# Token block sums in the layer before, weight sums ahead of the first eviction, first down weights as slots come free

## The chip, the cores and the metric

One NeuronCore of a Trainium2 chip. The metric is the device time of one execution in microseconds; the kernel before has a median of 3389.93 us over 3 runs (3389.51 to 3396.35). TensorE is PE in the profile, VectorE DVE, ScalarE ACT, GpSimd POOL, SyncE SP.

## The reference, cut to what matters

A stack of four transformer-like layers over 512 tokens of width 1024, in float32. Layers 0 and 1 are a mixer, a cross attention and a SwiGLU feed-forward network (FFN); a third layer (s) has another mixer and its own SwiGLU FFN; a fourth (t) has none. The part that the change touches:

```
def _swiglu(h, w_in, w_out):
    a, g = jnp.split(h @ w_in, 2, axis=-1)
    return (jax.nn.silu(a) * g) @ w_out
...
        x = x + _cross_attention(_rmsnorm(x, norm_xattn[l]), mem_n, xa_wq[l], xa_wkv[l], xa_wo[l])
        x = x + _swiglu(_rmsnorm(x, norm_ffn[l]), ffn_w_in[l], ffn_w_out[l])
```

The hidden width is 2816, that is 22 tiles of 128 (NH).

## The kernel before

Activations lie transposed, 8 tiles of 128 features by 512 tokens (X). Every float32 operand is split into a high part (rounded to fp32r) and the remainder, and a product is three matmuls: high x high, high x low, low x high (`unit_passes`, lines 318 to 320). Weights come in 527 units of 128 x 1024 through a ring of four raw tiles (RW, loaded by SP). ScalarE rounds a unit into WH (line 313, `w_hi`), GpSimd forms the remainder WL (line 3666), and WH and WL have three slots each (SPLIT). `w_hi(act, st, v)` rounds all units up to v that are not yet rounded; each waits for its raw tile and for its slot (`split_free`).

Each engine walks one list of stages in order (PLAN), so what stands behind a waiting instruction on its engine waits too. The stages around the change, for the FFN of layers 0 and 1 (f0, f1):

- `Linear("x0.o")` or `("x1.o")`: the output projection of the cross attention, 8 units j = 0 to 7, 24 matmuls each. VectorE adds each result into X ("eviction j", line 473); ScalarE squares X[j] (line 423), VectorE sums the squares (line 436).
- `Late`: ScalarE scales X by the norm's gain into XH (line 1234), VectorE forms XL (line 1244) and adds the last square (line 1254). The norm's reciprocal root is applied later, to the products.
- `Pairs(f.up, 2)`: the first two of 22 gate and up pairs, four ordinary units. The first starts tile by tile as XL comes (`pe_start`). Then the variance is summed on TensorE (line 1267), ScalarE takes the root (line 1276), VectorE the reciprocal (line 1284), scales each product (line 550) and multiplies gate by up (line 574, the "eviction" of a pair); ScalarE's SiLU is line 535.
- `Sevens`: the other 20 pairs by a scheme of Winograd's kind. The contraction is cut in two halves of 512 features, the tokens in two halves of 256 columns, a pair of weight units in the blocks A11, A12, A21, A22. Seven products per pair (A11, S1, S2, S4, S3, A12, A22, each 12 matmuls of 256 columns) replace eight. S1 to S4 are sums of weight blocks: VectorE forms S1, S2, S4 in PSUM banks 4 to 6 (`sums`, lines 788 to 792), GpSimd S3 in TERM (line 771). Each of the seven weight operands is rounded by ScalarE (line 759, `term_hi`); GpSimd forms the remainder of A11, S3, A12, A22 (line 774) and VectorE of S1, S2, S4 (line 779, `remainder`). The token operands of four products are sums of blocks of X (MIXED): `opening` on VectorE and `opening_act` on ScalarE form them, in two halves h of the contraction, each half as four sums `mix(t)` (line 690), four roundings (line 702) and four remainders (line 706, `mix_lo`). Half 0 needs X tiles 0, 1, 4, 5 and half 1 tiles 2, 3, 6, 7. Both halves stand at the head of `Pairs`, ahead of the root and the reciprocal. The weight sums of the first pair stand behind the first eviction of `Pairs` (`between(0)`), their remainders behind the second (`between(1)`). The bank of A11's result frees with the first eviction.
- `Down`: 22 units, each 24 matmuls over all eight banks. Its first units are rounded in `Sevens.scalar`: `ahead(m)` calls `w_hi` at m = 2 and 4 of the last pair, and once more stands behind the last SiLU. In `w_hi`, a unit of `Sevens` at index 3 or later returns at once (`if u - s7.u0 >= SPLIT: return`), and `st.unit`, the next unit to round, is moved past `Sevens` only behind the last SiLU.

The FFN of layer s (fs) has the same stages, except that its norm stands ahead (`late` is None): both halves of the sums stand at the head of `Pairs` too, and no reciprocal follows.

## Time and profile before

| | |
|---|---|
| median of 3 runs | 3389.93 us (3389.51 to 3396.35) |
| the profiled execution's own time | 3390.47 us |
| its span | 3388.7 us |
| TensorE busy | 3247.2 us, 96% |
| VectorE, ScalarE, GpSimd busy | 1720.6, 1424.4, 1447.8 us |
| mean granted clock | 0.986 |

Full speed of the clock (1.0) is 2.4 GHz, 0.5 is 1.2 GHz. Times in the rows are microseconds from the start of the span. In a timeline a row is the start, the duration, the engine, the line, the operation, output<-inputs, the shape and a count; in brackets stands how long the engine sat idle before and what released it. A row with a count over 1 runs from the start of its first to the end of its last instruction. TensorE's matmuls overlap, so the step from start to start is their pace (0.227 us for 512 columns and 0.12 for 256 at full clock), not the duration.

### The profile page before, as it was taken

Reading aid. Unit: us, or ns where it says so; the run is one execution under the profiler, and the core shown is the slowest. Engines: PE = TensorE matmul, PEld = TensorE weight load, DVE = VectorE, ACT = ScalarE, POOL = GpSimd, SP = SyncE. Lnnn points to the kernel's source line nnn. Section 1 sums busy time; section 2 is a strip of 40 time slices with the busy share of each in tenths; the row PEclk is TensorE's granted clock in tenths of the full one; section 3 lists DMA queues with packets and bytes.
Section 4 is the critical chain, followed back from the end, with each engine's and each line's share of the span. In section 5 each row is a group of like instructions: output and inputs, shape, how many; then the busy total and the mean of one; then the engine's idle time right before and its main releaser. Section 6 shows DMA issues by size and latency. Waiting matters only on the chain.

```text
span 3388.7 us, 47037 instructions
## 1 busy us (share of the span) xinstructions
PE 3247.2 (96%) x19536; PEld 2709.5 (80%) x19536; DVE 1720.6 (51%) x2631; ACT 1424.4 (42%) x2372; POOL 1447.8 (43%) x735
## 2 busy tenths in 40 slices
PE   8999989999999989999999998999899999999998
PEld 6778789987778789886677876998688778878887
DVE  8953478614443478513447655772373261134733
ACT  4543455423353455424434434553335432242332
POOL 5744256543354256543243023664344324414443
PEclk9999999999999999999999999999999999999999
DMA  4222123322232123333123031333232213212231
GB/s 165 87 94 94 50 81 107 104 96 94 69 106 94 50 82 112 101 100 104 55 84 117 20 107 63 109 104 100 81 118 94 69 56 100 87 38 97 96 124 69
DMA packets 83036, 302.88 MB, mean 89 GB/s; under 512 B 9060, under 2 KB 10888, under 8 KB 81928
## 3 DMA queue, kind: packets, MB, share of 16 engines
q1 hardware_dynamic: 78368, 280.55, 25.0%
q10 hardware_dynamic: 4456, 19.33, 1.5%
q8 instruction: 155, 2.54, 0.3%
q14 instruction: 57, 0.47, 0.0%
HBM read 290.39 MB, written 9.44 MB: 88 GB/s over the span
## 4 chain that ended last, share of the span: by engine, by line
PE 83%; DVE 8%; ACT 4%; issue 1%; POOL 0%; DVEq 0%; ACTq 0%
PE PS L318 23%; PE PS L319 22%; PE PS L320 22%; PE PS L1505 2%; PE PS L619 2%; PE PS L621 2%; PE PS L620 2%; PE PS L1626 1%; PE PS L2616 1%; DVE XL L1244 1%; DVE PS L690 1%; ACT WH L313 1%; PE PS L2608 1%; PE PS L1315 1%; PE PS L1491 1%
## 5 line engine op out<-in xcount | busy, mean ns | idle before, releaser
L3666 POOL TENSOR_TENSOR WL<-RW,WH 128x1024 fp32r<-128x1024 f32 x407 | 1005.2, 2473 | 1684.6 <-ACT WH L313 1684.1
L318 PE MATMUL PS<-XH,WH 128*128 128x512 f32 (+1 forms) x2728 | 1002.6, 368 | 50.8 <-POOL WL L774 16.5
L319 PE MATMUL PS<-XL,WH 128*128 128x512 f32 (+1 forms) x2728 | 993.0, 364 | 0.0
L320 PE MATMUL PS<-XH,WL 128*128 128x512 f32 (+1 forms) x2728 | 992.7, 364 | 0.0
L313 ACT ACTIVATE WH<-RW 128x1024 fp32r<-128x1024 f32 x407 | 427.0, 1053 | 590.1 <-PE PS L320 493.3
L318 PEld LDWEIGHTS PS<-XH,WH 128*128 128x128 f32 x2728 | 520.2, 191 | 152.1 <-issue 24.3
L320 PEld LDWEIGHTS PS<-XH,WL 128*128 128x128 f32 x2728 | 519.8, 191 | 80.2
L319 PEld LDWEIGHTS PS<-XL,WH 128*128 128x128 f32 x2728 | 520.4, 191 | 78.7 <-issue 2.2
L318 PE MATMUL PS<-YH,WH 128*128 128x512 f32 (+1 forms) x928 | 352.0, 379 | 17.8 <-POOL WL L3666 14.5
L319 PE MATMUL PS<-YL,WH 128*128 128x512 f32 (+1 forms) x928 | 350.8, 378 | 0.0
L320 PE MATMUL PS<-YH,WL 128*128 128x512 f32 (+1 forms) x928 | 350.3, 377 | 0.0
L318 PE MATMUL PS<-MIXED,WH 128*128 128x256 f32 x960 | 274.8, 286 | 6.7 <-DVE WL L779 6.7
L320 PE MATMUL PS<-MIXED,WL 128*128 128x256 f32 x960 | 274.4, 286 | 0.0
L319 PE MATMUL PS<-MIXED,WH 128*128 128x256 f32 x960 | 274.4, 286 | 0.0
L774 POOL TENSOR_TENSOR WL<-RW,WH 128x512 fp32r<-128x512 f32 x180 | 234.5, 1304 | 55.3 <-ACT WH L759 50.2
L318 PEld LDWEIGHTS PS<-YH,WH 128*128 128x128 f32 x928 | 176.5, 190 | 52.4 <-POOL WL L3666 17.6
L320 PEld LDWEIGHTS PS<-YH,WL 128*128 128x128 f32 x928 | 176.9, 191 | 31.7
L319 PEld LDWEIGHTS PS<-YL,WH 128*128 128x128 f32 x928 | 176.8, 190 | 31.1
L318 PEld LDWEIGHTS PS<-MIXED,WH 128*128 128x128 f32 x960 | 186.8, 195 | 7.5 <-DVE WL L779 7.5
L319 PEld LDWEIGHTS PS<-MIXED,WH 128*128 128x128 f32 x960 | 186.9, 195 | 0.0
L320 PEld LDWEIGHTS PS<-MIXED,WL 128*128 128x128 f32 x960 | 186.9, 195 | 0.0
L950 DVE TENSOR_TENSOR YL<-A,YH 128x512 fp32r<-128x512 f32 x66 | 47.9, 737 | 272.7 <-ACT YH L946 272.7
(583 smaller groups left out, 4436.8 us busy)
## 6 DMA issues: line engine op xcount, KB each, us to landing
RW<-in_units SPq DMA_DIRECT2D x527, 512.0 KB, 3.3
spill<-X ACTq DMA_DIRECT2D x2, 2048.0 KB, 6.6
X<-in_xT SPq DMA_DIRECT2D x8, 256.0 KB, 6.2
A<-spill ACTq DMA_DIRECT2D x1, 2048.0 KB, 7.8
X<-spill ACTq DMA_DIRECT2D x4, 512.0 KB, 5.7
X<-spill ACTq DMA_DIRECT2D x1, 2048.0 KB, 9.3
out_T<-X ACTq DMA_DIRECT2D x4, 512.0 KB, 3.0
spill<-X ACTq DMA_DIRECT2D x1, 1536.0 KB, 5.1
```

What stands on the lines that cost most here:

```text
L313: nc.scalar.activation(WH[:, u % SPLIT, :], RW[:, u % RAW, :], ACT.Copy).then_inc(split_hi, 1)
L318: mm(out, hi, xh, start=first, stop=False, skip_group_check=onto)
L319: mm(out, hi, xl, start=False, stop=False, skip_group_check=onto)
L320: return mm(out, lo, xh, start=False, stop=last, skip_group_check=onto)
L619: mm(o, xh, wh, start=(k == 0), stop=False)
L620: mm(o, xh, wl, start=False, stop=False)
L621: last = mm(o, xl, wh, start=False, stop=(k == KT - 1))
L690: st.do(nc.vector.scalar_tensor_tensor(out=self.part(out, h, k), in0=self.x(half, cols, k), scalar=self.gain_of(half, k), in1=self.part(ot ...
L774: nc.gpsimd.tensor_tensor(WLH[:, w, :], self.raw(p, m), WHH[:, w, :].bitcast(F32), ALU.subtract).then_inc(term_done, 1)
L950: st.do(nc.vector.tensor_tensor(YL[:, self.hslot(k), :], T(k), YH[:, self.hslot(k), :].bitcast(F32), ALU.subtract), f"{self.name}.lo{k}")
L1505: last = mm(PS[rows, 6 + n % 2, c0:S], value(j), self.pt_of(s, g)[:, j, c0:S], start=(j == 0), stop=(j == (TT if self.keys is None else se ...
L3666: nc.gpsimd.tensor_tensor(WL[:, u % SPLIT, :], RW[:, u % RAW, :], WH[:, u % SPLIT, :].bitcast(F32), ALU.subtract).then_inc(split_done, 1)
```

## The change

1. In layers 0 and 1, half 0 of the token block sums is formed in the `Linear` before, behind evictions 5 and 6 (`early`, `early_act`, hung on `outs[l].between` and `between_act`). The squares of that layer go to tiles 8 to 15, since the old ones lie under MIXED. In fs, `early` stays at the head of `Pairs`.
2. Half 1 is `finish`: at the head of `Pairs` in layers 0 and 1, behind the first eviction in fs. S1, S2, S4 of the first pair are formed in `finish` too: behind the root in layers 0 and 1, ahead of the reciprocal. The remainders of S1 and S2 stand behind the first eviction, that of S4 behind the second.
3. ScalarE rounds A11 and S1 ahead of the first pair's SiLU (`amid_act` is set, so `w_hi` is called ahead of it).
4. `st.unit` is moved past `Sevens` inside `ahead`, so the calls at m = 2 and 4 of the last pair round down units 0 and 1.

```
@@ Linear.vector @@
                     st.do(ins, f"ev{self.e0 + j}")
+                    if self.between is not None:
+                        self.between(st, j)
@@ Pairs.scalar @@
                         if self.of:
                             w_hi(act, st, u + SPLIT + self.eager)
+                        elif self.amid_act is not None:
+                            w_hi(act, st, u + SPLIT + (i == 0))
                         st.wait_ge(*reached(f"gated{e}"))
...
+                    if self.amid_act is not None:
+                        self.amid_act(st, i)
@@ Sevens @@
+            def early(self, st, j):
+                if j == 5:
+                    st.settle()
+                    self.mix(st, 0, 0)
+                    self.mix(st, 0, 1)
+                    self.mix_lo(st, 0, 0)
+                elif j == 6:
+                    st.settle()
+                    self.mix(st, 0, 2)
+                    self.mix(st, 0, 3)
+                    for t in (1, 2, 3):
+                        self.mix_lo(st, 0, t)
+
+            def early_act(self, st, j):
+                if j == 5:
+                    self.right_act(st, 0)
+                    self.mix_hi(st, 0, 0)
+                elif j == 6:
+                    for t in (2, 1, 3):
+                        self.mix_hi(st, 0, t)
+
+            def finish(self, st):
+                st.settle()
+                self.mix(st, 1, 0)
+                self.mix(st, 1, 1)
+                if self.late is None:
+                    self.sum_one(st, 0)
+                self.mix_lo(st, 1, 0)
+                st.settle()
+                self.mix(st, 1, 2)
+                self.mix(st, 1, 3)
+                for t in (1, 2, 3):
+                    self.mix_lo(st, 1, t)
+                if self.late is not None:
+                    st.wait_ge(*reached(f"{self.late.id}.std"))
+                    self.sum_one(st, 0)
+                self.sum_two(st, 0)
+                self.sum_four(st, 0)
+
+            def finish_act(self, st):
+                self.right_act(st, 1)
+                for t in (0, 2, 1, 3):
+                    self.mix_hi(st, 1, t)
...
             def opening(self, st):
-                for h in range(2):
-                    self.mix(st, h, 0)
-                    self.mix(st, h, 1)
-                    self.mix_lo(st, h, 0)
-                    st.settle()
-                    self.mix(st, h, 2)
-                    self.mix(st, h, 3)
-                    for t in (2, 1, 3):
-                        self.mix_lo(st, h, t)
-                    st.settle()
+                if self.late is None:
+                    for j in (5, 6):
+                        self.early(st, j)
+                else:
+                    self.finish(st)
...
+            def amid_act(self, st, i):
+                if i == 0 and self.late is None:
+                    self.finish_act(st)
+
             def between(self, st, i):
-                if i == 0:
-                    self.sums(st, 0)
-                elif i == 1:
+                if i == 0 and self.late is None:
+                    self.finish(st)
+                if i == self.first - 2:
+                    self.remainder(st, 0, self.S1)
+                    self.remainder(st, 0, self.S2)
+                elif i == self.first - 1:
+                    self.remainder(st, 0, self.S4)
                     if self.late is not None:
                         st.do(nc.vector.tensor_copy(bank(self.RSTD), self.late.r))
-                    for m in (self.S1, self.S2, self.S4):
-                        self.remainder(st, 0, m)
@@ Sevens.scalar, ahead @@
                         elif m in (2, 4):
+                            st.unit = max(st.unit, self.u0 + 2 * self.n)
                             w_hi(act, st, self.u0 + 2 * self.n + m // 2 - 1)
@@ xattn @@
-            o = Linear(f"x{l}.o", add=True, ready=f"xo{l}", squares=20, summing=KT - 1)
+            o = outs[l] = Linear(f"x{l}.o", add=True, ready=f"xo{l}", squares=8, summing=KT - 1)
@@ ffn @@
+            if late is not None:
+                outs[l].between, outs[l].between_act = s7.early, s7.early_act
```

TensorE's, GpSimd's and SyncE's orders stay as they are. VectorE's order at the end of x0.o and the head of f0.up, before:

```order
L473 TENSOR_TENSOR X<-X,PS 128x512
L436 TENSOR_TENSOR SD<-SD,A 128x512
L1244 SCALAR_TENSOR_TENSOR XL<-X,VEC,XH 128x512 x4
L473 TENSOR_TENSOR X<-X,PS 128x512
L1244 SCALAR_TENSOR_TENSOR XL<-X,VEC,XH 128x512 x4
L1254 TENSOR_TENSOR SD<-SD,A 128x512
L690 SCALAR_TENSOR_TENSOR PS<-X,VEC,PS 128x256 x4
L706 TENSOR_TENSOR MIXED<-PS,MIXED 128x512
L690 SCALAR_TENSOR_TENSOR PS<-X,VEC,PS 128x256 x4
L706 TENSOR_TENSOR MIXED<-PS,MIXED 128x512 x3
```

The same place in the changed kernel, from eviction 5 on (line 690 is now 696, 706 is 713, 1244 is 1307):

```order
L473 TENSOR_TENSOR X<-X,PS 128x512
L696 SCALAR_TENSOR_TENSOR PS<-X,VEC,PS 128x256 x4
L713 TENSOR_TENSOR MIXED<-PS,MIXED 128x512
L436 TENSOR_TENSOR SD<-SD,A 128x512
L473 TENSOR_TENSOR X<-X,PS 128x512
L696 SCALAR_TENSOR_TENSOR PS<-X,VEC,PS 128x256 x4
L713 TENSOR_TENSOR MIXED<-PS,MIXED 128x512 x3
L436 TENSOR_TENSOR SD<-SD,A 128x512
L1307 SCALAR_TENSOR_TENSOR XL<-X,VEC,XH 128x512 x4
L473 TENSOR_TENSOR X<-X,PS 128x512
L1307 SCALAR_TENSOR_TENSOR XL<-X,VEC,XH 128x512 x4
```

Eight sums and four remainders stand between evictions 5 and 7 now. ScalarE's order from the root to the second SiLU in f0.up, before and then in the changed kernel (L1276 and L1339 are the root, L535 and L539 the SiLU, L759 and L813 the rounding of a weight operand: from RW it is A11, from PS S1, S2, S4):

```order
L1276 ACTIVATE NR<-PS,CST 128x512
L535 ACT_TABLE_LOAD
L535 ACTIVATE SG<-SG 128x512
L759 ACTIVATE WH<-RW 128x512
L759 ACTIVATE WH<-PS 128x512
L535 ACTIVATE SG<-SG 128x512
```

```order
L1339 ACTIVATE NR<-PS,CST 128x512
L813 ACTIVATE WH<-RW 128x512
L813 ACTIVATE WH<-PS 128x512
L539 ACT_TABLE_LOAD
L539 ACTIVATE SG<-SG 128x512
L813 ACTIVATE WH<-PS 128x512 x2
L539 ACTIVATE SG<-SG 128x512
```

A11 and S1 moved ahead of the first SiLU. ScalarE's order at the end of `Sevens` in f0, before and then in the changed kernel (L853 and L916 are the last copy of a result, L859 and L922 the last SiLU, L313 the rounding of down units):

```order
L853 ACTIVATE SG<-PS 128x256
L859 ACTIVATE SG<-SG 128x512
L313 ACTIVATE WH<-RW 128x1024 x3
```

```order
L916 ACTIVATE SG<-PS 128x256
L313 ACTIVATE WH<-RW 128x1024 x2
L922 ACTIVATE SG<-SG 128x512
L313 ACTIVATE WH<-RW 128x1024
```

Two of the three roundings moved ahead of the last SiLU. The same rows stand in f1 and fs.

## Rows read from the trace of the kernel before

**Rows 1.** The page, part 1: busy us, share of the span, instructions.
```profile
PE 3247.2 (96%) x19536; PEld 2709.5 (80%) x19536; DVE 1720.6 (51%) x2631; ACT 1424.4 (42%) x2372; POOL 1447.8 (43%) x735
```

**Rows 2.** Waits of TensorE: us in total, times, longest us.
```profile
PE PS L318 <- POOL WL L3666: 17.2, 9, 3.9
PE PS L318 <- POOL WL L774: 16.5, 3, 7.5
...
PE PS L318 <- DVE WL L779: 6.7, 3, 2.3
```

**Rows 3.** Timeline of TensorE, head of f0's seven-product stage: start, duration, instruction, idle before.
```profile
438.94 0.39 PE L320 MATMUL PS<-XH,WL 128*128 128x512 f32 x1
446.80 0.58 PE L318 MATMUL PS<-XH,WH 128*128 128x256 f32 x1 [7.46 <-POOL WL L774]
...
452.06 0.58 PE L318 MATMUL PS<-MIXED,WH 128*128 128x256 f32 x1 [2.34 <-DVE WL L779]
```

**Rows 4.** Windows: length, busy us (count) of PE, PEld, DVE, ACT, POOL; granted clock; DMA.
```profile
443.50:444.00 0.50, 0.00 (x0) 0.00 (x0) 0.50 (x1) 0.00 (x0) 0.00 (x0) 0.76 0.00 0
457.00:457.50 0.50, 0.50 (x4) 0.50 (x4) 0.00 (x0) 0.00 (x0) 0.50 (x2) 0.59 0.71 131
...
2107.00:2110.00 3.00, 2.78 (x23) 2.78 (x24) 2.83 (x5) 2.54 (x6) 2.59 (x2) 1.00 0.00 0
```

**Rows 5.** Timeline of VectorE around the same head.
```profile
413.35 4.38 DVE L1244 SCALAR_TENSOR_TENSOR XL<-X,VEC,XH 128x512 fp32r<-128x512 f32 x4 [0.87 <-ACT XH L1234]
...
418.25 2.73 DVE L1244 SCALAR_TENSOR_TENSOR XL<-X,VEC,XH 128x512 fp32r<-128x512 f32 x4
421.08 2.71 DVE L1254 TENSOR_TENSOR SD<-SD,A 128x512 f32<-128x512 f32 x1
423.82 1.79 DVE L690 SCALAR_TENSOR_TENSOR PS<-X,VEC,PS 128x256 f32<-128x256 f32 x4
426.28 0.69 DVE L706 TENSOR_TENSOR MIXED<-PS,MIXED 128x512 fp32r<-128x512 f32 x1 [0.67 <-ACT MIXED L702]
...
439.99 3.35 DVE L1284 RECIPROCAL NR<-NR 128x512 f32<-128x512 f32 x1 [1.27 <-ACT NR L1276]
443.47 1.29 DVE L550 TENSOR_TENSOR SG<-PS,NR 128x512 f32<-128x512 f32 x2
444.93 0.69 DVE L574 TENSOR_TENSOR A<-SG 128x512 f32<-128x512 f32 x1 [0.17 <-ACT SG L535]
```

**Rows 6.** Timeline of ScalarE around the same head.
```profile
406.22 1.04 ACT L313 ACTIVATE WH<-RW 128x1024 fp32r<-128x1024 f32 x1
...
439.20 0.69 ACT L1276 ACTIVATE NR<-PS,CST 128x512 f32<-128x512 f32 x1
...
464.79 0.38 ACT L847 ACTIVATE SG<-PS 128x256 f32<-128x256 f32 x1 [0.29 <-PE PS L320]
...
474.87 0.38 ACT L847 ACTIVATE SG<-PS 128x256 f32<-128x256 f32 x1 [0.29 <-PE PS L320]
```

**Rows 7.** Timeline of GpSimd around the same head.
```profile
420.77 2.47 POOL L3666 TENSOR_TENSOR WL<-RW,WH 128x1024 fp32r<-128x1024 f32 x1 [5.58 <-ACT WH L313]
```

**Rows 8.** Timeline of ScalarE, last pair of f0's seven-product stage.
```profile
649.11 0.39 ACT L853 ACTIVATE SG<-PS 128x256 f32<-128x256 f32 x1 [1.06 <-PE PS L320]
...
655.15 2.93 ACT L313 ACTIVATE WH<-RW 128x1024 fp32r<-128x1024 f32 x3
```

**Rows 9.** Timeline of TensorE, the same place.
```profile
654.55 0.28 PE L320 MATMUL PS<-MIXED,WL 128*128 128x256 f32 x1
658.69 0.72 PE L318 MATMUL PS<-YH,WH 128*128 128x512 f32 x1 [3.86 <-POOL WL L3666]
```

**Rows 10.** Timeline of VectorE, the same place: the last eviction.
```profile
656.34 0.41 DVE L899 TENSOR_TENSOR A<-SG,PS 128x256 f32<-128x256 f32 x1
```

**Rows 11.** Windows, same columns: f0's down projection, its first products.
```profile
662.00:662.50 0.50, 0.50 (x3) 0.36 (x3) 0.00 (x0) 0.00 (x0) 0.50 (x1) 0.79 1.02 205
```

**Rows 12.** Timeline of TensorE, first product of fs.down.
```profile
2310.74 0.72 PE L318 MATMUL PS<-YH,WH 128*128 128x512 f32 x1 [3.11 <-POOL WL L3666]
```

More of the change, by code:

```diff
@@ L699, in mix_act, with mix_hi @@
                     st.do(nc.scalar.activation(self.part(self.MIX_BANK[3], h, k), self.x(0, 1, k), ACT.Copy, scale=self.gain_of(0, k)), f"{self.name}.right{h}")
-                for t, read in ((0, 1), (2, 2), (1, 3), (3, 3)):
-                    st.wait(f"{self.name}.mix{read}.{h}")
-                    st.do(nc.scalar.activation(self.mixed_half(t, h, 0), bank(self.MIX_BANK[t]), ACT.Copy), f"{self.name}.mixhi{t}.{h}")
+            def mix_hi(self, st, h, t):
+                st.wait(f"{self.name}.mix{(1, 3, 2, 3)[t]}.{h}")
+                st.do(nc.scalar.activation(self.mixed_half(t, h, 0), bank(self.MIX_BANK[t]), ACT.Copy), f"{self.name}.mixhi{t}.{h}")
             def mix_lo(self, st, h, t):
@@ new lines, in finish_act @@
+            def finish_act(self, st):
+                self.right_act(st, 1)
+                for t in (0, 2, 1, 3):
+                    self.mix_hi(st, 1, t)
+            def opening(self, st):
+                if self.late is None:
[3 more added lines that the diff above has]
+                    self.finish(st)
+            def opening_act(self, st):
+                if self.late is None:
+                    for j in (5, 6):
+                        self.early_act(st, j)
+                else:
+                    self.finish_act(st)
@@ L1634, in xattn @@
             split(f"xo{l}", [T(28 + k) for k in range(KT)], XH, XL, ready=lambda k: f"xa{l}.o{k}")
-            o = Linear(f"x{l}.o", add=True, ready=f"xo{l}", squares=20, summing=KT - 1)
-            o.then = late(f"fn{l}", f"norm_ffn{l}", ready=lambda k: f"ev{o.e0 + k}", after=o.name, left=[KT - 1], sq=lambda i: T(20 + i))
+            o = outs[l] = Linear(f"x{l}.o", add=True, ready=f"xo{l}", squares=8, summing=KT - 1)
+            o.then = late(f"fn{l}", f"norm_ffn{l}", ready=lambda k: f"ev{o.e0 + k}", after=o.name, left=[KT - 1], sq=lambda i: T(8 + i))
             return o.then
@@ L1641, in keys @@
             return T(((14, 15, 36, 37), (4, 5, 6, 7))[l][j // 2])[:, (j % 2) * MEM:(j % 2 + 1) * MEM]
-        mix = {}
+        mix, outs = {}, {}
         def ffn(l, alpha=None, late=None, summed=False, weights=None, first=1):
@@ L1648, in ffn @@
             s7 = up.sevens = Sevens(f"f{l}.up", 2, NH - 2, at(0), ACT.Silu, None if late is None else f"norm_ffn{l}", late, f"fn{l}.biased7" if late is None else None)
-            up.opening, up.opening_act, up.between = s7.opening, s7.opening_act, s7.between
+            up.opening, up.opening_act, up.amid_act, up.between = s7.opening, s7.opening_act, s7.amid_act, s7.between
+            if late is not None:
+                outs[l].between, outs[l].between_act = s7.early, s7.early_act
             s7.then = Down(f"f{l}.down", up, alpha, summed, weights)
```

35 lines of the change are left out of this document (19 added, 16 removed).

## The prediction

> **What bounds the kernel now.** I read the page's busy shares first, then the waits of TensorE, then the timelines and clock windows at the two ends of the seven-product stages. TensorE is busy for 96% of the span [rows 1], so time is won only by closing its gaps, or by keeping its clock up. Nearly all of the largest gaps fed by GpSimd lie at two kinds of places, and the diff touches both [rows 2]. The first is the head of `Sevens`, where the first product (A11) waits for WL of line 774 (16.5 us in three waits, one in each FFN layer) and the second (S1) for the remainder of line 779 (6.7 us in three). The second is the head of `Down`: waits of 3.9 us in f0 and f1 (the longest of line 3666), and 3.11 us in fs [rows 12].
>
> In f0 the last matmul of the four up units starts at 438.94, A11 at 446.80 after 7.46 us idle, S1 at 452.06 after 2.34 more [rows 3]. The granted clock falls near 443.6 (0.76 is the mean of a half window at 2.4 GHz and at 1.2) and is back only near 457.3 [rows 4]. ScalarE's first copy of a pair comes right behind that pair's A11: 464.79 and 474.87 [rows 6], so a pair takes 10.08 us on TensorE. The second pair's A11 therefore started one seventh of 10.08 (1.44 us) before 464.7, at 463.3. From 438.94 to 463.3 are 24.4 us, for 10.1 of products: 7.9 us of step to A11, 2.3 of wait at S1, and 4.1 lost to the clock.
>
> Why A11 is late: VectorE works without a long pause from 413 to 445 (lows, both halves of the block sums, the reciprocal of 3.35 us, two scalings 1.29, the eviction at 444.93) [rows 5]. A11's weights were rounded by ScalarE only behind the first pair's SiLU, although they were in the raw ring long before.
>
> **The change, part by part: head of f0.** I carry the new order forward with before's durations.
>
> 1. Half 0 of the block sums goes behind evictions 5 and 6 of x0.o. ScalarE's rounding behind eviction 5 starts at 406.22 and occupies it to 407.2 [rows 6]; the two gain products then take 0.86, so VectorE starts at 408.1. One step (four 256-column sums, round, remainder) takes 3.15 us, from 423.82 to the end of 426.28+0.69 [rows 5], so to 411.3. The square sum and eviction 6 end at 412.6, the next four sums at 414.4, and the three remainders, since the new order asks for the one that ScalarE rounds second first, at 417.3. Then come a square sum (417.9), four lows at 0.68 each (420.7), eviction 7 (421.3) and four lows of 2.73 in all [rows 5], ending at 424.0; before they ended at 421.0. So the first up unit, which eats one low per 0.68 us, starts 2.8 us late, at 418.6, and ends **3.0 us later**, at 424.7. This is the price of the change.
>
> 2. VectorE's last square sum then meets GpSimd's WL of the third unit. Before, this sum took 2.71 us and ended 0.55 after GpSimd's 420.77+2.47 [rows 5, 7], while the sums of line 690, which read PSUM and one SBUF tile, ran 1.79 for four. So operations of VectorE with two SBUF operands wait for GpSimd here. It now ends at 426.8. The GPSIMD Engine Reference of the Trainium skill (Specifications) states the same, contention for the shared SBUF interfaces with VectorE instructions that have two SBUF inputs; by that rule, the trace agrees, and the moved sum S1 (two raw weight tiles) is exposed to it as well. A sum without it would put the reciprocal some 2 us earlier and be about 2 us better per layer.
>
> 3. Half 1 follows, 3.15 + 4.4 us, to 434.4. ScalarE rounds unit four (432.9, behind all of half 1, where before it stood between the halves), GpSimd takes some 2.4 [rows 7] and the fourth unit can start at 436.5, just 0.3 late. The square root follows the rounding and a table load of 1.3 us: it ends at 435.9 (439.9 before [rows 6]).
>
> 4. The weight sums S1, S2, S4 stand ahead of the reciprocal now: S1 waits for GpSimd until 436.5 and ends at 437.0, the others at 438.4. The reciprocal of 3.35 ends at 441.8 (443.3 before), so it gains little. The scalings take 1.29, and the eviction ends at 443.9 (445.6 before) [rows 5].
>
> 5. A11 no longer waits for the SiLU: rounded at 436.5, its WL is done at 439.5 behind GpSimd's TERM. What is late next is its bank, which frees with the first eviction: **A11 starts at 443.95**. TensorE ends unit four at 442.0, so it idles 2.0 us. S1's remainder follows the eviction directly, 444.6, and waits for nothing. S2 needs ScalarE's copy of A11, queued behind the second SiLU and two roundings: 1.1 us idle. The second pair starts at 443.95+10.08+1.1 = 455.1.
>
> 463.3 - 455.1 = **8.2 us in f0**. The same by terms: 7.9+2.3+4.1 go, 3.0+2.0+1.1 (and rounding) come. This takes the clock as staying up: in fs, behind idle of 1.6 and 2.0 us, it stood at 1.00 [rows 4]. The idle at the head of the up stage is 3.0 us, and could lower it there; but 0.9 us lost in unit one is covered by the 2.0 at A11. f1 has the same shape (its wait is the 7.5 of rows 2): 8.2 again. Bounds for a layer: 5 (the clock falls, another 1.8, and S1 or S2 slip by 1.4) and 10.2 (no idle at A11).
>
> **Head of fs.** This layer has no preceding `Linear` to take half 0. Half 1 goes behind the first eviction. Its waits are 16.5 less twice 7.5, 1.6 us, and 6.7 less 2.34 twice, 2.0. Unit four's weights are now rounded behind a table load and a SiLU, so that unit starts 1.6 late, in place of the 1.6 at A11; the sums are ready sooner, so most of the 2.0 goes. I take 2.0, bounds -1 and 3.6.
>
> **Tail of the seven-product stages.** ScalarE is done with its copies at 649.5 and then has only the last SiLU until 655.15, where the three roundings of down units stand in a row [rows 8]. The last product's last matmul starts at 654.55, the first of down at 658.69 [rows 9]. Now units 0 and 1 are rounded behind products 3 and 5 of the last pair. Unit 0: 649.4 to 650.4, GpSimd to 652.9, two us before TensorE asks; unit 1 is done at 655.5. Its lows are there, and the banks of the first nine passes are free; the next three (asked for at 656.7) want the last weighting, the others (at 657.4) the last eviction, which ends at 656.75 behind it [rows 10], so both come in time. So the step of 4.14 us becomes 0.12: 4.0 us. The clock fell during that gap and was back near 662.2 [rows 11]: 3.5 us at half rate, 1.8 to 1.9 us. **5.9 us each in f0 and f1**, bounds 4.0 and 5.9. In fs the wait is 3.11 [rows 12]: 3.3 + 1.7 = 5.0. GpSimd's WL of unit 1 may hold an eviction there by 1 us; down's banks 4 to 7 cover it with 2.7 us of passes.
>
> Down units 1 and 2 are ready in time, and everything behind shifts with TensorE. Instruction counts of TensorE, GpSimd and the DMA queue stay as they are; the squares move to other tiles at no cost.
>
> **Sum.** 2 x 8.2 + 2.0 + 2 x 5.9 + 5.0 = 35.2 us. The profiled execution took 3390.5 us (span 3388.7 and 1.8 around it), 0.5 above the median of the runs: 3390.5 - 35.2 = 3355.3, and I say 3355.
>
> **The rivals.**
> A: the heads pay less, since the clock falls in the new gaps after all. For it: the wait of 3.9 us at down's head was enough [rows 9, 11], and the new gaps are 3.0 and 2.0. Against: fs [rows 4]. Price 1.8 per fall plus slips, 2 to 4 in each of f0 and f1: 3359 to 3363. The page TensorE: Matmul & The Clock Gate of the Trainium skill (Why this matters for your kernels) warns of idle gaps between bursts of matmuls for this reason.
> B: the heads pay nothing. Half 1, the weight sums and the reciprocal stand in one VectorE queue; if the early half costs more than the 3.0 us (evictions 6 and 7 held longer), the first eviction is no earlier than before and the gap just moves. Then only the tails pay, 16.8: 3374.
> C: the tails pay nothing, because the early roundings delay the copies and SiLU of the last pair or their raw tiles have not landed. ScalarE's free time from 649.5 on speaks against [rows 8]. Only the heads pay, 18.4: 3372.
> D, slower: the clock falls in the 3.0 us gap at the up stage and stays at 1.2 GHz through its four units. That is 4 x 24 matmuls of 0.227 us = 21.8 us more per layer, 43.6 for two, less the 35.2: 3399. It decides from 17.6 us of work at half rate per layer on. Low stretches here last 3.5 to 13.7 us, the latter with two further gaps inside [rows 3, 4, 11], which speaks against it.
>
> **How the numbers follow.** Forecast 0.68, A 0.20, B 0.06, C 0.04, D 0.02. The forecast's own range: heads 2 x (-2 to +2), fs head -3 to +1.6, tails to -4: 3349 to 3362 as a practical spread. With A it reaches 3364; B and C are left out, most of the 2 in 10, and I add 2 us for phases of the clock elsewhere that shift: 3347 to 3366. About 0.2% (7 us) is what this measurement can tell from no change. Forecast, A, B and C are all faster by more than that: 0.97, with 0.01 for the same (both B and C) and 0.02 slower.
>
> **What would show it.** The waits of TensorE on line 774's successor should fall from 16.5 to under 5 us, those at down's head be gone, the step to the first product of down be 0.12 us. The first up unit of f0 should start near 418.6 (a new wait of 3 us on VectorE's XL), A11 near 444, the second pair near 455, with the clock at 1.00. I am wrong if A11 starts after 446, if the clock falls there, or if down's head still shows a gap.

## The result and the profile after

| | before | after |
|---|---|---|
| median | 3390.44 us (3389.51 to 3396.35, 4 runs) | 3359.67 us (3358.76 to 3360.74, 4 runs) |
| the profiled execution's own time | 3390.47 us | 3360.74 us |
| its span | 3388.7 us | 3358.9 us |

The ratio is 0.9906, 95% interval 0.9889 to 0.9923: 30.8 us faster, where 35.2 were summed. The range, 3347 to 3366, held it; rival A's, 3359 to 3363, holds it as well, so the time alone does not choose between the forecast and A. A second measurement of the same kernel (below) gave 3357.78 us.

The page of the changed kernel, part 1, answers to [rows 1]:

```profile
PE 3239.8 (96%) x19536; PEld 2700.3 (80%) x19536; DVE 1716.6 (51%) x2631; ACT 1424.4 (42%) x2372; POOL 1450.7 (43%) x735
```

The same instructions, and on every engine nearly the same busy time. What went is idle time of TensorE. Its waits, as in [rows 2] (us in total, times, longest; L3731 was L3666, L833 was L779, L1307 was L1244, L580 was L574):

```profile
PE PS L318 <- DVE XL L1307: 21.2, 10, 10.0
...
PE PS L318 <- POOL WL L3731: 6.6, 6, 2.2
PE PS L318 <- DVE A L580: 3.6, 2, 1.8
...
PE PS L318 <- DVE WL L833: 1.1, 2, 0.7
```

The 16.5 us of line 774 are gone, and 10.6 of the 17.2 us of line 3666. New are 3.6 us for the first eviction, and the waits on XL (15.7 us in six on line 1244 before) are longer by about the 2.85 us in each of f0 and f1 that step 1 asked for.

**Head of f0.** Timeline of TensorE (start, duration, instruction, idle before and its releaser), against [rows 3]:

```profile
419.81 0.47 PE L318 MATMUL PS<-XH,WH 128*128 128x512 f32 x1 [2.85 <-DVE XL L1307]
...
442.85 0.39 PE L320 MATMUL PS<-XH,WL 128*128 128x512 f32 x1
445.06 0.36 PE L318 MATMUL PS<-XH,WH 128*128 128x256 f32 x1 [1.82 <-DVE A L580]
```

Timeline of VectorE, against [rows 5]:

```profile
413.81 1.80 DVE L696 SCALAR_TENSOR_TENSOR PS<-X,VEC,PS 128x256 f32<-128x256 f32 x4
416.38 1.89 DVE L713 TENSOR_TENSOR MIXED<-PS,MIXED 128x512 fp32r<-128x512 f32 x3 [0.78 <-ACT MIXED L709]
...
425.00 2.70 DVE L1317 TENSOR_TENSOR SD<-SD,A 128x512 f32<-128x512 f32 x1
...
436.83 1.00 DVE L839 SCALAR_TENSOR_TENSOR PS<-RW 128x512 f32<-128x512 f32 x1 [1.55 <-ACT NR L1339]
...
439.28 3.35 DVE L1347 RECIPROCAL NR<-NR 128x512 f32<-128x512 f32 x1
442.76 1.29 DVE L556 TENSOR_TENSOR SG<-PS,NR 128x512 f32<-128x512 f32 x2
444.22 0.69 DVE L580 TENSOR_TENSOR A<-SG 128x512 f32<-128x512 f32 x1 [0.17 <-ACT SG L539]
```

Timeline of GpSimd and of ScalarE, against [rows 7] and [rows 6]:

```profile
424.70 2.46 POOL L3731 TENSOR_TENSOR WL<-RW,WH 128x1024 fp32r<-128x1024 f32 x1 [6.84 <-ACT WH L313]
```

```profile
458.33 0.39 ACT L910 ACTIVATE SG<-PS 128x256 f32<-128x256 f32 x1 [0.29 <-PE PS L320]
```

Half 0 now stands between evictions 5 and 7, the first up unit waits 2.85 us, the square sum is held by GpSimd for 2.70 us again (it ends at 427.70, 0.54 after GpSimd's 424.70+2.46), and A11 waits for its bank. The second pair's first copy came at 464.79 and comes at 458.33.

**Tail of f0.** Timelines of ScalarE, GpSimd and TensorE, against [rows 8, 9]:

```profile
642.93 1.05 ACT L313 ACTIVATE WH<-RW 128x1024 fp32r<-128x1024 f32 x1
645.59 1.06 ACT L313 ACTIVATE WH<-RW 128x1024 fp32r<-128x1024 f32 x1 [1.61 <-PE PS L320]
648.16 0.63 ACT L922 ACTIVATE SG<-SG 128x512 f32<-128x512 f32 x1 [1.50 <-DVE SG L955]
```

```profile
644.06 5.07 POOL L3731 TENSOR_TENSOR WL<-RW,WH 128x1024 fp32r<-128x1024 f32 x2 [2.02 <-ACT WH L313]
```

```profile
648.09 0.28 PE L320 MATMUL PS<-MIXED,WL 128*128 128x256 f32 x1
648.21 0.40 PE L318 MATMUL PS<-YH,WH 128*128 128x512 f32 x1
```

Two units are rounded behind products of the last pair, GpSimd works on them while TensorE still multiplies, and the first product of down follows after 0.12 us, as forecast; the step was 4.14.

**An account by stages.** To see where time went, I take the same VectorE instruction in both traces, at a point before and a point behind each place, and subtract its times. How far the changed kernel is ahead, in us:

| place | ahead in front | ahead behind | won there | forecast |
|---|---|---|---|---|
| head of f0 | -1.2 | 6.4 | **7.6** | 8.2 |
| tail of f0 | 6.4 | 12.2 | **5.7** | 5.9 |
| head of f1 | 12.1 | 20.2 | **8.1** | 8.2 |
| tail of f1 | 20.2 | 25.9 | **5.7** | 5.9 |
| head of fs | 24.5 | 25.8 | **1.3** | 2.0 |
| tail of fs | 25.8 | 30.8 | **5.0** | 5.0 |
| sum | | | **33.4** | 35.2 |

The points are read to 0.1 us, so a row can be off by that.

What the places won is 33.4 us; the span is shorter by 29.8. The rest was given back between them, where no instruction was changed: 1.2 us before the first place (0.8 of it at 247 to 255 us, where the clock was low for 6.8 us, and before for 3.4), 1.4 between f1's tail and fs, in small steps that no single row explains, and 1.7 at 2650 to 2655 us of the changed kernel's trace, a low stretch that the kernel before did not have; 0.4 came back at the very end. This account holds for two executions. The interval of the ratio, 26 to 38 us, has room for 33.4 and for 35.2 as well.

### The profile page after: what moved, and what is told of

The parts are those of the page before. It is cut to its first block, busy times and chain, and to the rows that moved or that the text cites. A ratio compares the mean times of both kernels' runs of the same rounds, so it can differ in the third digit from the quotient of the medians.

```text
span 3358.9 us, 47090 instructions
## 1 busy us (share of the span) xinstructions
PE 3239.8 (96%) x19536; PEld 2700.3 (80%) x19536; DVE 1716.6 (51%) x2631; ACT 1424.4 (42%) x2372; POOL 1450.7 (43%) x735
## 4 chain that ended last, share of the span: by engine, by line
PE 83%; DVE 8%; ACT 3%; issue 1%; DVEq 0%; ACTq 0%
PE PS L318 23%; PE PS L320 22%; PE PS L319 22%; PE PS L1568 2%; PE PS L625 2%; PE PS L627 2%; PE PS L626 2%; PE PS L2681 1%; PE PS L1689 1%; PE PS L2673 1%; PE PS L1378 1%; PE PS L1554 1%; ACT WH L313 1%; DVE XL L1307 1%; PE PS L3357 1%
## 5 line engine op out<-in xcount | busy, mean ns | idle before, releaser
L3731 POOL TENSOR_TENSOR WL<-RW,WH 128x1024 fp32r<-128x1024 f32 x407 | 1006.5, 2476 | 1678.3 <-ACT WH L313 1677.8
L313 ACT ACTIVATE WH<-RW 128x1024 fp32r<-128x1024 f32 x407 | 427.7, 1054 | 593.5 <-PE PS L320 496.8
```

The source lines that it names most:

```text
L313: nc.scalar.activation(WH[:, u % SPLIT, :], RW[:, u % RAW, :], ACT.Copy).then_inc(split_hi, 1)
L3731: nc.gpsimd.tensor_tensor(WL[:, u % SPLIT, :], RW[:, u % RAW, :], WH[:, u % SPLIT, :].bitcast(F32), ALU.subtract).then_inc(split_done, 1)
```

## The experiments

In all the runs the kernel before was measured beside the others: 3392.1, 3391.81 and 3391.18 us for the three groups. Ratios are to it. "Head" and "tail" gains are by the account above. Theories of the expectations: A is the prediction's, B its rival.

**1. The tails alone** (the kernel before with one line):

```
                         elif m in (2, 4):
+                            st.unit = max(st.unit, self.u0 + 2 * self.n)
                             w_hi(act, st, self.u0 + 2 * self.n + m // 2 - 1)
```

> The kernel before with one line of the change: the unit counter is moved past the seven-product stage inside `ahead`, so that down units 0 and 1 are rounded behind products 3 and 5 of the last pair. My theory (each part pays where it stands): the tails alone give 5.7 us in f0, 5.75 in f1 and 5.2 in fs as the trace of the changed kernel shows, 16.7 in all, so 0.9951 of before (about 3373.7). The three steps to down's first matmul are 0.12 to 0.25 us and the clock stays at 1.00 there, while the waits of 7.5 us at the two heads stay. Rival (most of it is the heads, and the tails' gain is given back by clock falls elsewhere): under 12 us.

3379.52 us (3378.89 to 3380.97), ratio 0.9961 (0.9948 to 0.9973): 12.6 us faster, by the interval 9.2 to 17.6. By stages the three tails win 5.7, 5.7 and 5.0, 16.4 together: all of what was expected. Windows of its clock (length, busy us and count of PE, PEld, DVE, ACT, POOL, granted clock, DMA):

```profile
1618.00:1629.00 11.00, 10.09 (x32) 6.02 (x33) 7.76 (x20) 5.14 (x21) 0.00 (x0) 0.53 0.06 21
2096.00:2104.00 8.00, 6.07 (x33) 5.77 (x33) 5.57 (x9) 4.91 (x11) 5.08 (x4) 0.57 0.13 35
```

The second is the head of fs, which this edit leaves as it was, and where the clock of the kernel before stood at 1.00 [rows 4]: 2.0 us are lost there. The first costs 2.7. It goes the other way too: the head of f0 is not touched either, and there the clock was low for 6.8 us in place of 13.7, which gave 2.3 us. So the price of the tails was right, and its profiled execution (10.4 us shorter by span) is short of it by low clock elsewhere. The median, 12.6, lies between the expected 16.7 and the rival's "under 12", and its interval holds both; it is the stage gains that speak for the theory.

**2. The heads alone** (the changed kernel without that line):

> The changed kernel without that line: heads alone. Theory: 7.6 us in f0, 9.6 in f1, 0.8 in fs, 18.0 in all, 0.9947 of before; the waits of 3.9, 3.9 and 3.1 us at down's heads stand as before, and e1 and e2 add up to the whole change plus what the clock takes elsewhere (34.8 by stages against 29.8 in the spans). Rival (the two parts help each other, for example by the clock): their gains add up to clearly less than 30.8.

3377.8 us (3374.11 to 3381.07), ratio 0.9956 (0.9943 to 0.9968): 14.3 us faster, by the interval 11 to 19. The heads win 7.6, 8.1 and 1.3 us, 17.0 together; 9.6 had been expected for f1 and 0.8 for fs. The tails of f0 and f1 win nothing, and that of fs loses 1.2: the clock is low there for 6.8 us, before for 3.4. The stage gains of the two halves, 16.4 and 17.0, add up to the 33.4 of the whole; their medians do so only within their intervals (12.6 + 14.3 = 26.9, against 30.8). Rival C falls by run 1, rival B by this one.

**3. Half 0 back at the head of the up stage** in f0 and f1; the rest of the change stays:

```
             def opening(self, st):
-                if self.late is None:
-                    for j in (5, 6):
-                        self.early(st, j)
-                else:
+                for j in (5, 6):
+                    self.early(st, j)
+                if self.late is not None:
                     self.finish(st)
...
-            if late is not None:
-                outs[l].between, outs[l].between_act = s7.early, s7.early_act
```

(and alike for ScalarE, with unit four rounded between the halves)

> The changed kernel with half 0 of the token block sums of f0 and f1 put back to the head of the up stage (between the lows and half 1), all else kept: the first weight sums ahead of the reciprocal, A11 and S1 rounded ahead of the first SiLU. Theory A (VectorE's queue is what bounds the heads): half 0 costs VectorE some 7.5 us there, of which only the 3 us by which the first up unit starts sooner come back to TensorE, and these do not count since the fourth unit then only waits longer for the first eviction. The first eviction of f0 moves from 444.9 to about 449, A11 with it, idle before A11 8 to 9 us instead of 1.8, and the clock falls there: 5 to 7 us slower than the changed kernel in each of f0 and f1, 10 to 14 in all. Theory B (the early half gives nothing, the order at the first SiLU is what pays): within 3 us of the changed kernel.

3369.96 us (3367.8 to 3370.64), ratio 0.993 (0.9916 to 0.9943), 10.3 us slower than the changed kernel. TensorE at the head of f0:

```profile
449.06 0.55 PE L318 MATMUL PS<-XH,WH 128*128 128x256 f32 x1 [9.09 <-DVE A L580]
```

The heads of f0 and f1 lose 5.8 and 6.0 us against the changed kernel: theory A holds (5 to 7 in each), B is refuted. With the shift in front of the place taken off, A11 comes 4.5 us later in both layers; a low stretch of 10.2 us, where the changed kernel has 3.4 in f0 and none in f1, goes with the rest. These 4.5 us are the 7.5 us of half 0 less the 3.0 that step 1 had put as its price. The weight sums ahead of the eviction, without the early half, make A11's wait longer than it ever was (9.1 us against 7.5): they lengthen the queue of VectorE. The early half is what pays for them.

**4. Only part of half 0 early.** The sums behind eviction 6 are moved behind the lows; those behind eviction 5 stay.

```
+                if self.late is not None:
+                    self.early(st, 6)
...
-                outs[l].between, outs[l].between_act = s7.early, s7.early_act
+                outs[l].between = lambda st, j: s7.early(st, j) if j == 5 else None
+                outs[l].between_act = lambda st, j: s7.early_act(st, j) if j == 5 else None
```

(and alike for ScalarE, with unit four rounded ahead of half 1)

> The changed kernel with the second part of half 0 (four sums, three roundings, three remainders, about 4.4 us of VectorE) moved from behind eviction 6 to behind the lows in f0 and f1; the first part stays behind eviction 5. Theory A (VectorE's queue sets the first eviction, TensorE's 2.9 us of idle at the head of the up stage is covered): the idle at the up stage's head goes to about 0, but the work of VectorE between eviction 5 and the first eviction stays the same, so A11 moves by no more than 2 us either way and the idle there grows from 1.8 to about 4.5 us; the clock may fall for longer. Time within 4 us of the changed kernel, rather slower. Theory B (the late start of the up stage is a real price): 2 x 2.9 = about 6 us faster than the changed kernel.

3365.71 us (3365.17 to 3367.86), ratio 0.9921 (0.9907 to 0.9934), 6.0 us slower than the changed kernel: A's "rather slower" with a size beyond its 4, and B, faster, refuted. The up stage waits 1.59 us in place of 2.85, not about 0 as A had it, and A11 waits the more, 5.92 us where A said 4.5:

```profile
417.74 0.47 PE L318 MATMUL PS<-XH,WH 128*128 128x512 f32 x1 [1.59 <-DVE XL L1312]
...
447.10 0.55 PE L318 MATMUL PS<-XH,WH 128*128 128x256 f32 x1 [5.92 <-DVE A L580]
```

The 2.85 us wait in front of the up stage is worth its price: of the 4.4 us of VectorE's work that were moved to behind the lows, 2.8 reach A11 in both layers. The rest does not, since the lows, which start sooner, now meet GpSimd. VectorE and GpSimd here, and VectorE in the changed kernel:

```profile
415.22 4.36 DVE L1312 SCALAR_TENSOR_TENSOR XL<-X,VEC,XH 128x512 fp32r<-128x512 f32 x4 [0.87 <-ACT XH L1302]
```

```profile
414.65 2.39 POOL L3737 TENSOR_TENSOR WL<-RW,WH 128x1024 fp32r<-128x1024 f32 x1 [4.56 <-ACT WH L313]
```

```profile
418.92 2.74 DVE L1307 SCALAR_TENSOR_TENSOR XL<-X,VEC,XH 128x512 fp32r<-128x512 f32 x4
```

The first low ends 0.55 us after GpSimd's operation and takes 2.37 us of the 4.36, as the square sum is held in step 2 of the prediction; the same stood in the kernel before (4.38 us for four [rows 5]), and the early half takes the lows out of GpSimd's way. The heads lose 2.9 and 3.5 us.

**5. Sums S2 and S4 behind the first eviction** in f0 and f1:

```
-                self.sum_two(st, 0)
-                self.sum_four(st, 0)
+                else:
+                    self.sum_two(st, 0)
+                    self.sum_four(st, 0)
...
+                    if self.late is not None:
+                        self.sum_two(st, 0)
+                        self.sum_four(st, 0)
```

> The changed kernel with the second and third weight sum of f0's and f1's first pair (1.4 us of VectorE) moved from ahead of the reciprocal to behind the first eviction and the remainder of S1. Theory A (VectorE's queue bounds the whole head, not only A11): the first eviction comes 1.4 us sooner and the idle of 1.8 us at A11 shrinks to about 0.4, but the remainders of S2 and S4 come 1.5 us later than they would and TensorE waits there instead, 0.4 us at S2 and about 1.2 at S4: no gain in f1, and at most the 1.8 us of the clock in f0. Within 2 us of the changed kernel. Theory B (A11's bank is the only thing that is late): 1.4 us per layer, and the clock stays up in f0: 3 to 5 us faster.

3364.19 us (3362.19 to 3364.9), ratio 0.9917 (0.9902 to 0.9932), 4.5 us slower than the changed kernel by medians whose intervals overlap. A11 no longer waits, the third product (S2) does. TensorE and the first eviction on VectorE, and a window:

```profile
443.30 0.28 PE L318 MATMUL PS<-XH,WH 128*128 128x256 f32 x1
...
448.69 0.35 PE L318 MATMUL PS<-MIXED,WH 128*128 128x256 f32 x1 [2.36 <-DVE WL L838]
```

```profile
441.78 0.69 DVE L580 TENSOR_TENSOR A<-SG 128x512 f32<-128x512 f32 x1 [0.17 <-ACT SG L539]
```

```profile
420.00:424.00 4.00, 4.00 (x12) 3.12 (x11) 4.00 (x7) 2.80 (x5) 0.20 (x1) 0.57 0.01 4
```

That A11 does not wait at all is in part the clock's doing: it was low in the up stage in both layers, so TensorE came later to A11. The eviction ended 0.83 us ahead of A11, where 0.15 is the distance when A11 waits for it, so its bank was free 0.7 us before TensorE came. Where the changed kernel's clock fell at the same place, A11's wait was 1.1 us shorter for it (0.70 in place of 1.80, run 8), so with the clock up a wait of about 0.4 would have been left here (an estimate), as A had it. The wait at S2, 2.36 us, is above A's 0.4 there and 1.2 at S4 together; S4 waits for nothing.

By stages the two heads lose only 0.2 and 0.7 us, within A's 2 us. The profiled execution, the fastest of the four, is behind the changed kernel's by 1.5 us of span, 0.9 of it at these heads; the rest of the 4.5 us between the medians is not explained by the edit. That it would gain (B) is refuted.

**6 and 7. A short delay at the start.** The changed kernel with two (then four) copies of ScalarE put ahead of its first rounding, 1.1 (2.2) us, nothing else:

```
+                raw_landed(st, 0)
+                for k in range(2):
+                    nc.scalar.activation(SG[:, k, :], RW[:, 0, 0:S], ACT.Copy)
```

> The changed kernel with two extra ScalarE copies of 128x512 (1.1 us) ahead of the first rounding, so that all that follows starts 1.1 us later and nothing else is changed. Theory (where the clock falls among the gaps depends on when in the execution they lie; that took about 5 us of the 34.8 us that the stages gave): the time differs from the changed kernel by something else than 1.1 us, up to 6 us either way, and the low stretches lie at other gaps, while stage by stage the steps with the clock at 1.00 are the same. Rival (the clock falls at the same gaps whatever their time): 1.1 us slower within 1 us, same low stretches.

> The same with four copies, 2.2 us. Theory: again other low stretches, a time that does not follow the delay (between 3357 and 3367). Rival: 2.2 us slower than the changed kernel and 1.1 slower than the run before it, same low stretches.

3359.26 us (3358.25 to 3361.84), ratio 0.9902 (0.9886 to 0.9919), and 3361.74 us (3359.77 to 3362.61), ratio 0.991 (0.9895 to 0.9925). Against the trace of run 8 below, the same program without the copies, the first is 1.0 us late at 60 us, then 3.0 at 403, 4.6 at 805, 2.0 at 2060 and 1.8 at 3300; the second 2.0, 1.7, 3.8, 1.4 and 1.3. By medians the first is 0.4 us under the changed kernel's first result, where the rival had 1.1 above it within 1 us; the second is 2.1 above, the rival's 2.2, and 4.0 above run 8. The rival's "same low stretches" is refuted in both: the first trace has two, at 365.1 and 423.2 us, that neither trace of the changed kernel has. The delay is there at the start and then drowns in jumps of 1 to 3 us, up and down, which lie where one execution has a low stretch and the other none. Whether the delay itself chose these stretches, the two runs cannot say; run 8 shows that none is needed.

**8. The changed kernel once more**, unaltered:

> The changed kernel once more, unaltered, beside the three that follow on the same chip. Theory A (the changed kernel's own time repeats within about 2 us): 3358 to 3362, ratio to the kernel before 0.990 to 0.992. Theory B (a few us of every result are the accident of which gaps the clock fell in during one measurement, so that a repeat wanders too): more than 3 us away from 3359.7.

3357.78 us (3354.71 to 3359.92), ratio 0.9899 (0.9883 to 0.9916). By the median A holds (just under its range), but single executions of one unaltered program range over 5 us. Beside the kernel before in this group, 3391.18 us, the gain is 33.4 us, what the account by places had summed. Three stretches by window, first in the first trace of the changed kernel:

```profile
445.50:449.50 4.00, 4.00 (x23) 4.00 (x22) 3.73 (x8) 2.46 (x5) 1.53 (x2) 0.57 0.00 0
1162.00:1166.00 4.00, 3.84 (x18) 2.75 (x16) 3.95 (x7) 2.80 (x6) 0.24 (x1) 1.00 0.00 0
2039.00:2046.00 7.00, 4.98 (x15) 1.26 (x16) 5.30 (x9) 4.62 (x9) 2.49 (x1) 1.00 0.20 77
```

and in this one, the same program:

```profile
445.50:449.50 4.00, 3.33 (x28) 3.15 (x28) 3.72 (x7) 3.26 (x7) 2.06 (x2) 1.00 0.00 0
1162.00:1166.00 4.00, 4.00 (x13) 3.13 (x12) 4.00 (x7) 2.81 (x5) 0.02 (x1) 0.57 0.00 0
2039.00:2046.00 7.00, 5.74 (x16) 1.45 (x16) 4.72 (x8) 6.10 (x9) 0.77 (x1) 0.53 0.22 75
```

All three changed sides. (Run 8 was measured on the chip of runs 9, 10 and 12, the first trace in another measurement; that the chip alone does not decide it is seen on this chip itself, in the last section.) At 1162 to 1166 us the clock fell behind the new wait in front of f1's up stage, and it cost nothing: TensorE came later to A11 and waited less there, while A11 started at the same point of VectorE's order. TensorE in f1, the first trace and then this one:

```profile
1186.11 0.36 PE L318 MATMUL PS<-XH,WH 128*128 128x256 f32 x1 [1.80 <-DVE A L580]
```

```profile
1186.35 0.36 PE L318 MATMUL PS<-XH,WH 128*128 128x256 f32 x1 [0.70 <-DVE A L580]
```

In f0, where the clock stayed up this time, the third product (S2) shows the wait that the prediction had put at 1.1 us. TensorE, and ScalarE's copy of A11's result:

```profile
448.30 0.36 PE L318 MATMUL PS<-MIXED,WH 128*128 128x256 f32 x1 [0.67 <-DVE WL L833]
```

```profile
447.79 0.36 ACT L910 ACTIVATE SG<-PS 128x256 f32<-128x256 f32 x1
```

The row names a remainder of VectorE, but the one that ended last (448.24) is S4's, for which S2 does not wait. By the kernel S2 waits for ScalarE's copy, as the prediction said: it ends at 448.15, 0.15 us ahead of the product, the same distance as from the first eviction to A11.

With the clock low (the first trace) it is absent, since the products come later than their operands. So the fall in f0 costs only 0.5 us by the account, not the 1.7 of its 3.4 us at half rate. Run 10 has the same in f1: the clock fell behind A11 there, and by the account this head loses 0.5 us against the first trace.

**9. The remainders in another order** (2, 1, 3 in place of 1, 2, 3, in both halves):

```
-                    for t in (1, 2, 3):
+                    for t in (2, 1, 3):
                         self.mix_lo(st, 0, t)
```

> The changed kernel with only this altered: the remainders of the token block sums are formed in the order 2, 1, 3, so that block 2's, which A11's sum reads first, is there one VectorE operation sooner. By the stage account of the run with both edits, A11's wait at each FFN head falls from 1.8 to about 0.7 us: theory A, 1.5 to 3 us faster than the changed kernel, 3357 to 3358. Theory B (the 2.7 us between the changed kernel and that run were the clock's accident, not the edit): within 1 us of the changed kernel in this same call.

3357.69 us (3356.19 to 3360.88), ratio 0.9903 (0.9888 to 0.9918): the same as run 8. TensorE at f0's up stage and at A11:

```profile
418.76 0.47 PE L318 MATMUL PS<-XH,WH 128*128 128x512 f32 x1 [2.37 <-DVE XL L1307]
...
444.00 0.36 PE L318 MATMUL PS<-XH,WH 128*128 128x256 f32 x1 [1.82 <-DVE A L580]
```

My stage reading was wrong. The 0.7 us at A11, seen in the run with both edits, came of a fall of the clock at 422 to 426 in it, as in f1 of run 8. The order buys 0.5 us at the up stage of f0 and of f1 (2.37 against 2.85), because ScalarE rounds block 2 second, and by the account 0.6 us at the head of fs, where unit four waits 1.38 us in place of 1.69; 1.6 us in all is below what the medians tell.

**10. Unit four's weights early in fs:**

```
+                        if i == 0 and self.amid_act is not None:
+                            w_hi(act, st, u + SPLIT)
```

> The changed kernel with only this altered: in the last layer's second FFN stage (about 2100 us) the fourth up unit's weights are rounded by GpSimd before the first SiLU instead of amid the stage. Stage account: the wait of 1.7 us on that rounding before unit four goes and turns up at the first weight sum, so that the head pays nothing: theory A, 3359 to 3361, within 1 us of the changed kernel. Theory B (a wait on GpSimd costs only at unit four, the sum has slack): 1.4 to 1.7 us faster than the changed kernel, 3358.

3358.89 us (3356.22 to 3360.09), ratio 0.9904 (0.989 to 0.9919), the same again. The changed kernel waited for unit four's weights in fs:

```profile
2073.19 0.50 PE L318 MATMUL PS<-XH,WH 128*128 128x512 f32 x1 [1.69 <-POOL WL L3731]
```

Now A11 waits in its place, for GpSimd's remainder:

```profile
2076.60 0.39 PE L318 MATMUL PS<-XH,WH 128*128 128x256 f32 x1 [1.79 <-POOL WL L830]
```

Theory A in its sum: the wait taken from one product goes to another, and by the account the head loses 0.1 us. It goes to A11, though, which reads no weight sum, and not to the first weight sum as A had it; and it is ScalarE that rounds the unit, where the expectation says GpSimd. Both waits are on GpSimd's remainders, which speaks for its queue as the bound of this head.

**11 and 12. Both edits**, in the group of runs 5 to 7 and again beside run 8:

> The changed kernel with two edits: in all three FFN layers the block sums' remainders are formed in the order 2, 1, 3, in which ScalarE rounds them, in place of 1, 2, 3 (0.67 us less for VectorE at each of two places in f0 and f1 and two in fs); and in fs the fourth up unit is rounded ahead of the first SiLU and its table load. Theory A: VectorE's chain to the first eviction is 1.3 us shorter in f0 and f1, the idle at A11 goes from 1.8 to about 0.5 and the clock need not fall in f0; in fs the wait of 1.7 us for that unit's weights goes, and part of it comes back at A11 behind the shorter VectorE chain. Together 3 to 6 us faster than the changed kernel, less or more by what the clock does elsewhere. Theory B (these heads are bound by something else): no change beyond 1 us.

> Both edits once more (order 2, 1, 3 and the fourth unit's weights early), beside the changed kernel on the same chip. Theory A (the edit pays): 1.5 to 3.5 us below the changed kernel of this call, about 3357. Theory B: within 1 us of it.

3357.02 us (3355.96 to 3361.12), ratio 0.9899 (0.9884 to 0.9914), and 3358.25 us (3356.04 to 3360.47), ratio 0.9904 (0.9889 to 0.9918). The first lies 2.7 us under the first result of the changed kernel, and would pass for a gain; beside the changed kernel on one chip the second lies 0.5 us above it. Both theories A (3 to 6, then 1.5 to 3.5 us) fall. By stages the order's 0.5 us is there in f0 and fs of both, too small for the medians. No version was found that beats the changed kernel by more than the measurement tells.

## Why the prediction was right, step by step

- **Step 1** said that the early half costs 3.0 us in front of the up stage: the row says 2.85. The trace of after runs 1.2 us late from before this place on; with that taken off, the first product stands at 418.6, the time forecast. Without the early half, A11 is 4.5 us later (run 3), the 7.5 us of half 0 less that price, and with its second part behind the lows 2.8 (run 4).
- **Step 2**, the square sum held by GpSimd: 2.71 us before, 2.70 after. The comparison that the step drew, with the four sums of line 690, tests nothing: they start at 423.82, when GpSimd's operation had ended at 423.24. The changed kernel has rows that do, at the second pair, VectorE and then GpSimd:

```profile
449.48 1.65 DVE L839 SCALAR_TENSOR_TENSOR PS<-RW 128x512 f32<-128x512 f32 x1
451.24 0.70 DVE L844 SCALAR_TENSOR_TENSOR PS<-PS,RW 128x512 f32<-128x512 f32 x1
```

```profile
449.28 2.99 POOL L828 TENSOR_TENSOR WL<-RW,WH 128x512 fp32r<-128x512 f32 x2
```

  Both sums ran while GpSimd worked; S1's, of two SBUF tiles, took 1.65 us, and S2's, of PSUM and one SBUF tile, 0.70. In the first pair S1's sum took 1.00, and 0.70 in run 4, where GpSimd was idle for most of it: held a little, as the step said. What it waited for is ScalarE's root (idle of 1.55 us), where step 4 had named GpSimd.
- **Step 3**, the root's end at 435.9: ScalarE's row ends at 436.80, less 1.2 is 435.6.
- **Step 4**, the reciprocal's end at 441.8: 442.63 less 1.2 is 441.5. **Step 5**, A11 at 443.95 behind the first eviction: 445.06 less 1.2 is 443.9, idle 1.8 where 2.0 was said. That the bank bounds A11 is shown by the distance from the end of the first eviction to A11's start, 0.15 us in both layers of both traces and of runs 3 and 4, whose waits are 9.1 and 5.9 us; in run 5, where the eviction comes sooner, A11 starts without a wait, though in part because TensorE came late.
- **"This takes the clock as staying up"** is the sentence that failed, by the prediction's own sign of being wrong: in f0 the clock fell at 445.8 behind idle of 1.8 us, as rival A has it; in the second trace it did not behind 1.79 us, but fell at the up stage of f1. It is the rule more than the exception: the changed kernel and the variants that leave these heads or alter them little (runs 2 and 6 to 12) give nine traces, so 18 heads of f0 and f1; 7 have a fall of 3.4 us behind A11's wait, 7 one at the up stage, 4 none. What kept the time near the forecast is the price, which rival A mis-sized: it took 1.8 us per fall and slips on top; the difference between the two traces is 0.5, since a fall uses up the wait at the third product, 0.67 us here, and other slack. The fall at the up stage costs nothing, as step 5 had argued for its 0.9 us. Rival D's half clock lasts 3.4 us in these heads, and never through the four units.
- **Head of fs**: 1.3 where 2.0 was said, within the bounds. Unit four waits 1.69 us (1.6 forecast); run 10 shows that rounding it earlier on ScalarE only moves the wait to A11.
- **Tails**: 5.7, 5.7 and 5.0 against 5.9, 5.9 and 5.0. The step of 0.12 us and the clock at full speed behind it (no low stretch at 645 to 655) are both there. Run 1 gives the same three numbers in another kernel.
- **What the sum lacked** is a term for the clock outside the touched places. I added 2 us to the range for it and nothing to the sum. In the profiled executions it took 3.6 us (33.4 by places, 29.8 by span), 6 in run 1 and 7.6 in run 2 (whose profiled execution was the slowest of its five). It isn't a price of the change alone: two executions of one program differ by 1 to 3 us at single places and by up to 5 in time. The repeat's 33.4 us (28 to 40 by its interval) suggest that most of the missing 4.4 us of the first result was this scatter; what the sum itself has too much is 1.8 us by places, 0.6 at f0's head, 0.1 at f1's, 0.7 at fs's, 0.4 at the tails.
- **The range** has slips of its own. The bounds of a layer's head, 5 and 10.2, are -3.2 and +2.0 around 8.2, where the range took -2 and +2, and the terms that it lists add up to 3366 on the slow side, where it says 3362. No result depends on them, but that its ends held is weaker support than it looks.

Open stays whether the program before loses less to its clock than the changed one on average. Every profiled execution of a variant was short of its sum by places, but the kernel before gave one trace only. The records point that way. Outside the six places the clock was low for 59.2 us in the trace before, for 68.5 and 78.3 in the two of the changed kernel, and for 64.8 to 81.9 in the others. And run 1's five executions have a mean granted clock of 0.985, that of the 23 of the kernel before, although the falls of 3.4 us at the tails are gone from its trace. So part of the low time that a change removes seems to come back elsewhere. By the two traces it is 9 to 19 us more, which at half rate costs at most 5 to 10 us (an estimate), and less where TensorE would have waited anyway.

## What to carry to other kernels

Follow the queue of the engine that bounds the place (here VectorE, from the lows to the first eviction) and count each operation of it at its measured length; work taken out ahead of the deadline pays for most of its length, even where it opens a smaller wait in a cheaper place (4.5 us of 7.5 at A11 in run 3, 2.8 of 4.4 in run 4). Judge an edit of a few us by the stage in the trace, not by the medians of separate measurements: 2.7 us of apparent gain vanished beside its control. And before reading a shorter wait as a gain, see whether TensorE merely arrived later because its clock was low.

## What was not expected of the hardware

The same program, executed twice, had its clock at 1.2 GHz in different places: at 445.5 to 449.5 us (0.57 against 1.00), 1162 to 1166 (1.00 against 0.57), 2039 to 2046 (1.00 against 0.53), while others (783 to 787, 2405 to 2423) fell in both. Idle of 1.82 us in front of A11 was followed by a fall in one trace, idle of 1.79 us in the same place by none in the other. Over the nine traces A11 waited 1.77 to 1.83 us eleven times, and the clock fell behind seven of these waits; on the one chip of run 8 and run 12, in f0, it stayed up behind 1.79 us and fell at 444.3 behind 1.79 us. The Trainium skill's page TensorE: Matmul & The Clock Gate (Why this matters for your kernels) warns of idle gaps for the clock; these rows show that the gap alone does not decide it. What does was not found.
